# Alternating the two column halves inside each half-size projection product

## What is computed

```
h = rms_norm(x, norm_g[i])                    # 1056 tokens x 1024
z = h @ W_in                                  # layer 0: 1024 x 4096, layer 1: 1024 x 7168
y = [branch(z) * silu(gate), memattn(z) * silu(mgate)] @ W_out
x = x + y
```

## Time and profile before

| | us |
|---|---|
| median of 3 runs | 2362.45 |
| lowest and highest | 2357.27, 2372.4 |
| the profiled execution's own time | 2366.67 |
| its span, from first to last instruction | 2365.0 |
| PE busy | 2199.8 |
| PE weight loads busy | 1830.6 |
| DVE busy | 1292.2 |
| ACT busy | 1009.7 |

### The profile page before, as it was taken

How to read it: one execution, slowest core, us unless ns; L and a number is a source line. 1 busy time by engine, 2 the same in 40 slices (tenths; PEclk the granted TensorE clock), 3 DMA queues, 4 the chain that set the end, 5 groups by cost and what they waited for, 6 DMA issues and landing times. The chain is left out here.

```text
span 2365.0 us, 47114 instructions
## 1 busy us (share of the span) xinstructions
PE 2199.8 (93%) x18709; PEld 1830.6 (77%) x18709; DVE 1292.2 (55%) x2040; ACT 1009.7 (43%) x2091; POOL 431.6 (18%) x542
## 2 busy tenths in 40 slices
PE   6799999988999689999999997789999999997999
PEld 6799899866688589999999996566666656653787
DVE  6846667525423364334444442488888888874211
ACT  6534223224311144333233343347777777775100
POOL 0533223102000033222222220221121111100000
PEclk9899999998899899999999999889999999999999
DMA  8322222144635643334533326679999999977431
GB/s 266 104 88 86 80 63 68 60 169 165 213 106 149 180 148 110 101 109 128 155 112 89 109 92 241 217 273 374 398 407 394 406 398 388 377 274 281 137 107 54
DMA packets 287705, 453.97 MB, mean 192 GB/s; under 512 B 35554, under 2 KB 212654, under 8 KB 287470
## 3 DMA queue, kind: packets, MB, share of 16 engines
q1 hardware_dynamic: 279422, 421.60, 51.1%
q0 software_dynamic: 8064, 29.36, 3.3%
HBM read 373.02 MB, written 78.43 MB: 191 GB/s over the span
## 5 line engine op out<-in xcount | busy, mean ns | idle before, releaser
L233 DVE TENSOR_TENSOR h_w_lo<-l_w,h_w_hi 128x512 fp32r<-128x512 f32 x264 | 213.8, 811 | 219.1 <-ACT h_w_hi L226 216.7
L226 ACT ACTIVATE h_w_hi<-l_w 128x512 fp32r<-128x512 f32 x264 | 166.6, 633 | 241.9 <-PE i_c L322 85.8
L320 PE MATMUL i_x<-h_t_hi,h_w_hi 128*128 128x264 f32 x560 | 162.6, 290 | 6.1 <-DVE h_t_lo L279 5.5
L2885 PEld LDWEIGHTS b_krow<-ar_arena,b_qd 128*32 128x32 f32 x3072 | 107.0, 111 | 73.6 <-issue 58.2
L320 PE MATMUL i_y<-h_t_hi,h_w_hi 128*128 128x264 f32 x560 | 161.3, 288 | 0.0
L322 PE MATMUL i_x<-h_t_hi,h_w_lo 128*128 128x264 f32 x560 | 160.3, 286 | 0.0
L321 PE MATMUL i_x<-h_t_lo,h_w_hi 128*128 128x264 f32 x560 | 159.7, 285 | 0.0
L192 POOL TENSOR_TENSOR h_w_lo_full<-l_w 128x512 f32<-128x512 f32 x44 | 58.0, 1318 | 554.9 <-DMA l_w<-in_w_in_sb_dram 232.0
L321 PE MATMUL i_y<-h_t_lo,h_w_hi 128*128 128x264 f32 x560 | 159.0, 284 | 0.0
L322 PE MATMUL i_y<-h_t_hi,h_w_lo 128*128 128x264 f32 x560 | 158.9, 284 | 0.0
L320 PE MATMUL i_c<-h_t_hi,h_w_hi 128*128 128x264 f32 x448 | 130.0, 290 | 20.8 <-DVE h_t_lo L279 17.4
(11 more groups left out here) (365 smaller groups left out, 6415.4 us busy)
## 6 DMA issues: line engine op xcount, KB each, us to landing
ar_arena<-in_cache_sb_k_dram SPq DMA_DIRECT2D x73, 768.0 KB, 9.5
bf_vpage<-in_cache_sb_v_dram SPq DMA_DIRECT2D x64, 768.0 KB, 9.2
b_vpage<-in_cache_sb_v_dram SPq DMA_DIRECT2D x64, 768.0 KB, 8.4
l_w<-in_w_in_sb_dram SPq DMA_DIRECT2D x56, 512.0 KB, 4.4
l_w<-in_cache_sb_k_dram SPq DMA_DIRECT2D x36, 768.0 KB, 9.6
l_w<-in_w_in_pool_dram SPq DMA_DIRECT2D x32, 512.0 KB, 4.2
bf_kpage<-in_cache_sb_k_dram SPq DMA_DIRECT2D x19, 768.0 KB, 9.5
ar_arena<-scratch_yT SPq DMA_DIRECT2D x14, 1024.0 KB, 6.9
```

Of the source, the lines that this page charges most:

```text
L226: act.activation(self.w_hi[:, i % RING, :, :], self.source(i), ACT.Copy).then_inc(self.high, 1)
L233: dve.tensor_tensor(self.w_lo[:, i % RING, :, :], self.source(i), self.w_hi[:, i % RING, :, :].bitcast(F32), ALU.subtract).then_inc(self.r ...
L320: pe.matmul(out, w_hi, t_hi, start=kk == 0 and x in ("P1", "P2", "P5"), stop=False, skip_group_check=True)
L2885: ins = pe.matmul(krow[pair * CT:(pair + 1) * CT, 0:P], qd[:, i % 2, at:at + CT], kt[u % 2][:, h, f, :], start=odd == 0 and f == 0, stop=o ...
```

## The change

The loop over the two halves `n` moves from outside to inside. Before, half 0 gets all its 12 matmuls, then half 1. After, each of the 12 pairs of a weight tile and a token tile kind is issued for half 0 and then at once for half 1. The number of matmuls, their shapes, operands and sums are the same. All waits of a product, for both halves, now stand ahead of its first matmul. The two halves become done at the 23rd and the 24th matmul; before it was at the 12th and the 24th.

```diff
--- before.py
+++ after.py
@@ -313,14 +313,15 @@
                 pe.wait_ge(self.copied, self.copy_at[p, {"P6": "P1", "P3": "P5", "P7": "P6"}[x]] + n + 1)
             if x == "P4":
                 pe.wait_ge(self.added, self.add_at[p, "P7"] + n + 1)
-            out, cols = self.bank(p, x)[n][:, 0:SUB], slice(n * SUB, (n + 1) * SUB)
-            for kk in range(K2):
-                w_hi, w_lo = self.w_hi[:, i % RING, kk, :], self.w_lo[:, i % RING, kk, :]
-                t_hi, t_lo = self.hi[t][:, kk, cols], self.lo[t][:, kk, cols]
-                pe.matmul(out, w_hi, t_hi, start=kk == 0 and x in ("P1", "P2", "P5"), stop=False, skip_group_check=True)
-                pe.matmul(out, w_hi, t_lo, start=False, stop=False, skip_group_check=True)
-                ins = pe.matmul(out, w_lo, t_hi, start=False, stop=kk == K2 - 1, skip_group_check=True)
-            ins.then_inc(self.done, 1)
+        for kk in range(K2):
+            w_hi, w_lo = self.w_hi[:, i % RING, kk, :], self.w_lo[:, i % RING, kk, :]
+            for m, (w_part, t_part) in enumerate(((w_hi, self.hi[t]), (w_hi, self.lo[t]), (w_lo, self.hi[t]))):
+                for n in range(2):
+                    out, cols = self.bank(p, x)[n][:, 0:SUB], slice(n * SUB, (n + 1) * SUB)
+                    ins = pe.matmul(out, w_part, t_part[:, kk, cols], start=kk + m == 0 and x in ("P1", "P2", "P5"),
+                                    stop=kk == K2 - 1 and m == 2, skip_group_check=True)
+                    if kk == K2 - 1 and m == 2:
+                        ins.then_inc(self.done, 1)
```

## The result

The median of 20 runs after the change is 2377.08 us (2370.55 to 2383.38), against 2364.66 us (2357.27 to 2372.4) for 20 runs before. The ratio is 1.0044, with a 95% interval of 1.0035 to 1.0054: by this ratio the change costs 10.4 us, from 8.3 to 12.8. The two medians themselves lie 12.4 us apart, inside the same interval. The forecast was +3.8 us.

The account below looks back on a forecast made before the run. Dense stages were taken as bound by PE's matmul count times start distance, stage starts by token preparation on ACT and DVE. Terms 1.0 + 1.0 + 1.3 + 0.34 + 0.15 = 3.8 us gave 2366.3 us, range 2356 to 2377.

Parts of the forecast that it names:

- the 1 ns allowed for the new order: Range allowance: the distance between matmul starts may move 1 ns either way through the new order alone, 7.4 us.
- (a): Matmuls in the products: more bank changes and repeated weight tiles, no weight load saved; distance of starts unchanged, cost nothing.
- sign of an error in (a): Profile check: a product taking 2.7 or 3.1 us instead of 2.91 would show the unchanged matmul distance was wrong.
- (b): Dense stage: half 0's copies and additions come later, but 2.1 us of room remain before the bank's next use; cost nothing.
- (c): End of each stage: the last P4 waits for both additions after P7; +1.0 us per stage, bounds 0.9 to 1.2.
- (d): Start of the pool phase: P5 of pairs 0 and 1 wait for both halves; +1.3 us, bounds 0.35 to 1.7.
- (e): Start of the in phase: P5 of pair 1 waits for the second addition; +0.34 us, bounds 0.2 to 1.5.
- (f): Behind the last product: the last copy ends later and the in phase's end waits for it; +0.15 us.
- The repeated weight tile pays: Rival, products: 2464 new weight tile repeats save at most 11 ns each, 27 us less, 2339 us; chance 0.08.
- Each bank change pays: Rival, products: 6776 new bank changes cost 9 ns each, 61 us more, 2427 us; chance 0.08.
- The steady state stalls: Rival, dense stage: PE waits where room is missing, 28 pairs at 0.3 us, 8 us, 2375 us; chance 0.06.

Follow-up runs that it names:

- bank_alone: Against before: output bank alternates at every matmul, operands in the old order, all waits ahead, both halves done at the end; 2364.51 us in one run.
- no_repeat: Against before: the last two matmuls of each inner tile exchanged, so no weight tile repeats inside an inner tile; 2371.09 us in one run.
- one_tile: Against after: every matmul reads the first rounded weight tile and its half's first rounded token tile; 2357.5 us in one run.
- late_done: Against before: same matmul order, but all waits ahead of the product and both halves told done by the last two matmuls; 2368.94 us, ratio 1.0019.
- dense_only: Against after: pair 0 and the last pair's P7 and P4 of each stage keep the order of before; 2372.17 us, ratio 1.0015 to before.
- operands_alone: Against after: operands alternate likewise, but the output bank changes only once, in the middle of the product; 2378.1 us in one run.
- groups3_dense: Against before: halves alternate after each three matmuls, except in pair 0 and the last P7 and P4; 2362.37 us, ratio 0.9996.

## Why the prediction came out as it did

The direction, the smallness and most terms were right. The median of after, 2377.08, lies right at the upper edge of the range, 2377, and that the range reaches so far is partly luck: the 1 ns allowed for the new order had no reason behind it and stood in no term. On the other side the median of before, with 20 runs, is 2.2 us above the one that the forecast started from. The size was off by 6.6 us by the ratio, and one term carries most of it.

**(a), the step that was mis-sized.** It said that the matmuls themselves cost nothing more. They cost 0.76 ns each in the pool phase and 0.66 in the in phase: 2688 x 0.76 + 4704 x 0.66 = 5.1 us. The reasons given for "nothing" held for the two causes that were weighed: the bank change is free (`bank_alone`) and the repeat of a tile has no price (`no_repeat`, `one_tile`). What was missing was a third cause, the order in which the two column halves and the inner tiles are read. The range allowed 1 ns for the new order, and the measured 0.7 fell in it; but with a sum made from zero it stood in no term. The prediction's own sign of an error in (a), 2.7 or 3.1 us for a product, was too coarse: the product went from 2.91 to 2.93 us, and that is already 5 us in 308 products. The trace of before had a hint in it: the earlier trace rows show one distance of 0.13 us where the mean is 0.121, and place by place the mean distances run from 117 to 127 ns, repeated from product to product within 1 or 2 ns at most places. A pattern that repeats like this can belong to the order, and a new order can have another mean; it need not, as `bank_alone` and `no_repeat` show.

**(b), room in the dense stretch**: right. PE waits nowhere in it for a copy or an addition; the bank in the example is free at 411.25 and its next user starts at 413.45, so 2.2 us are left where 2.1 was forecast. `late_done` and `bank_alone` have late handover everywhere and the distance of before.

**(c), the last P4**: +1.0 us in each stage as forecast, gone in `dense_only`.

**(d), the pool phase's start**: forecast +1.3 with bounds of 0.35 and 1.7; measured 1.64 in the one profile of after. P5 of pair 0 is late by 1.17 exactly as worked out. Other traces with the same waits there show how little the 1.64 is a fixed price: from DVE's first row to P5 of pair 1 it is 24.20 us in before, 25.83 in after, and only 24.67 in `late_done` and 24.64 in `operands_alone`, +0.47 and +0.44. In these two P5 of pair 0 took 4.4 us and not the 5.4 of after, with a granted clock of 0.73 and 0.74 in its first 6 us where after has 0.51, so P1 and what follows came sooner.

**(e), the in phase's start**: DVE's first row moved from 821.47 to 832.24, by 10.77 us, all of it from what lies ahead of this stage, and P5 of pair 1 from 856.08 to 867.20, by 11.12: +0.35 against 0.34. `late_done` and `operands_alone` have the same +0.33 and +0.34. A part came on top that the prediction didn't have. P5 of pair 1 ran at the low clock from its start, and the distance fell from 0.22 to 0.12 us after 3.8 us in before and after some 5.6 us in after. In `late_done` it falls late as well, and its dense stretch is 581.60 us in place of 580.70, with before's distance; 0.9 us of after's 4.4 are of this kind. Most of the other 3.5 are some 4,100 distances inside products at 0.66 ns more, the rest lies where one product follows another. The late fall is not a mark of the change's waits: `dense_only`, with pair 0 as in before, has 25 low-clock distances there, and `operands_alone`, with all waits ahead, has 15. Over the 14 traces, the stretch opened at the low clock (15 to 27 distances) in the seven where PE had been idle for 3.4 to 3.7 us ahead of it, and at the full clock in the seven with 0.85 to 1.1 us.

**(f), the last copies**: from the last matmul's start to the instruction that ACT takes up behind the copies it is 0.60 us in before (1442.52 to 1443.12) and 0.75 in after (1459.11 to 1459.86): +0.15 as forecast.

Sum of what the traces show: 5.1 for the distance, 2.0 for the two ends, 1.6 and 0.35 for the two starts, 0.15 for (f), 9.2 us in all, within the measured 8.3 to 12.8; with the 0.45 of `late_done` for the pool phase's start it is 8.0, a little below. So 1.2 to 2.4 us to the middle are not explained. In the profiled execution of after PE waits 1.4 us longer for the mixer's saved state in the pool phase than in that of before. These rows (total us, times, the longest) are of before and of after:

```profile
PE p_aux L1245 <- DMA p_state<-in_state_pool_dram: 5.4, 3, 2.1
```
```profile
PE p_aux L1246 <- DMA p_state<-in_state_pool_dram: 6.8, 3, 2.7
```

Behind the longest of these waits, 2.7 us, after has some ten more distances at the low clock (0.84 granted from 364 to 375 us) where before has 1.00 from 359 to 370. With the nine of the in phase that is 1.9 us more at the low clock. A single profile cannot charge this to the change: `no_repeat`, with the halves and the waits of before, has 0.84 behind each of its three waits of this kind.

One sum of the prediction is a little off: its bounds of (c) to (f) add up to 2.5 and 5.75 us, not 2.4 and 5.9. And it said that a measurement tells about 1%; with 20 runs the interval was 0.1% to either side.

**The rivals.** "The repeated weight tile pays" is false: `no_repeat` takes the 8 repeats away and changes 0.04 ns. The Trainium skill's formula for the gap of an isolated matmul ("TensorE: Matmul & The Clock Gate", Back-to-back issue gap) gives 112.5 ns for 264 columns, an estimate from that page. Even `one_tile`, whose operand tiles never change within a half, stays at 120.06, with a weight load for each matmul, so the trace shows that the figure can't be used for this stream, in which every matmul has its load. "Each bank change pays" is false by `bank_alone`. "The steady state stalls" is false by the window of after, and in the pool phase by its list of waits: between P5 of pair 1 and the last P7, PE waits only for the mixer's saved state.

**Left open.** Which property of the read order sets the distance was not found. The bank doesn't matter, nor does it matter which kinds of tile (rounded or remainder) follow each other inside an inner tile. The sequence of column half and inner tile does matter, and so does the cut of the columns. No kernel changes the order of the weight tiles without that of the token columns, so the two streams of reads are not told apart. Whether this is the place of tiles in SBUF or something in TensorE's own pipeline, no run here tells.

## What to carry to other kernels

Where a stage is a dense stream of matmuls, look at the distances between starts place by place before the order is changed: if they repeat as a pattern, a reordering with the same work may move their mean. Here it moved by half a per cent either way, and a single profile showed it where a dozen timed runs hardly did. Before two stretches are compared, count their low-clock distances: a rounded clock of 1.00 hid 1.6 us between before and `groups3_dense`. When independent sums are interleaved, they all end late: count who waits at the ends of the stage, where no work stands between producer and user. To take such a change apart, keep its waits and drop its order, and the reverse; then let the output bank and the operands change one without the other.

## What the runs showed of the hardware

- Changing the PSUM bank with each matmul costs nothing: 121.54 ns with 22 changes more in a product, 121.54 without.
- A weight tile used by consecutive matmuls is loaded each time, 188 ns in the record, and a stream with one tile pair per half still has 120.06 ns between starts of 264 columns. At the low clock the distance is 0.22 us, which is 264 columns at 1.2 GHz; half of that is 110 ns, 10 less than the 120.06.
- The same 24 matmuls take from 120.9 to 122.2 ns each in the in phase by the order of their operands alone, with a pattern along the product that repeats (117 to 127 ns in before).
- Where PE had been idle for 3.46 us (before) or 3.66 us (after), the granted clock was 0.72 and 0.53 in the next 6 us; after 0.85 us of idle time (`groups3_dense`) it was 1.00.
